# Up projection of the gated MLP by Strassen's scheme: seven block products, two phases of 1024 tokens, and normed rows that pass through DRAM

## The reference

```python
mix = (gates[..., :D_MODEL] * y_a + gates[..., D_MODEL:] * y_b) @ w_out[l]
h = h + _rms_norm(mix, norm_mix_post[l])
hn = _rms_norm(h, norm_ffn_pre[l])
up = hn @ ffn_w_up[l]                                  # (2064, 1024) @ (1024, 5632)
a = _causal_dwconv(up[..., :D_FF], ffn_conv_w[l], ffn_conv_b[l])   # 3 taps over tokens
f = (jax.nn.gelu(a, approximate=True) * up[..., D_FF:]) @ ffn_w_down[l]
h = h + _rms_norm(f, norm_ffn_post[l])
return h[:, N_META:, :]
```

## Time and profile before

| | |
|---|---|
| Median of 3 runs | 3570.68 us (3565.49 to 3570.95) |
| Span of the profiled execution, first to last instruction | 3565.1 us |
| What lies around the span | not printed by itself; against the three runs, 0.4 to 5.9 us |
| PE busy | 3324.0 us, 93% of the span |
| PEld busy | 2995.8 us, 84% |
| DVE busy | 1443.1 us, 40% |
| ACT busy | 994.6 us, 28% |
| Mean granted clock of TensorE | 0.965 of 2.4 GHz |
| up stage | from 2073 us to 3067 us of the span |

### The profile page before, as it was taken

The page is one execution under the profiler, slowest core; times in us unless marked ns, Lnnn a source line. Parts: engine busy times, 40 slices in busy tenths (PEclk is TensorE's granted clock), DMA queues, the critical chain, the costliest instruction groups (busy, mean ns, idle before and its releaser), DMA issues. The chain is left out here.

```text
span 3565.1 us, 67387 instructions
## 1 busy us (share of the span) xinstructions
PE 3324.0 (93%) x26926; PEld 2995.8 (84%) x26926; DVE 1443.1 (40%) x2535; ACT 994.6 (28%) x1549; POOL 121.3 (3%) x126
## 2 busy tenths in 40 slices
PE   6999999999775888869989989999999999999998
PEld 6999999999654777769988879999999999788887
DVE  6566642222295566654444442222222222311433
ACT  5211123343472444441113331111111111211311
POOL 0000000000001222210000000000000000000000
PEclk8999999999877999989999999999999999999999
DMA  5233344334484334333335411111111111311432
GB/s 158 88 122 114 114 138 125 121 123 127 148 291 118 89 91 96 86 132 127 101 123 147 124 66 47 47 47 47 47 47 47 47 47 38 139 49 49 136 117 93
DMA packets 300638, 357.67 MB, mean 100 GB/s; under 512 B 133600, under 2 KB 246112, under 8 KB 291856
## 3 DMA queue, kind: packets, MB, share of 16 engines
q1 hardware_dynamic: 300560, 356.59, 31.9%
HBM read 221.52 MB, written 135.00 MB: 100 GB/s over the span
## 5 line engine op out<-in xcount | busy, mean ns | idle before, releaser
L432 PE MATMUL psum<-x_hi,proj_w_hi 128*128 128x344 f32 x1632 | 534.9, 328 | 4.7 <-DVE proj_w_lo L519 4.7
L432 PE MATMUL psum<-x_lo,proj_w_hi 128*128 128x344 f32 x1632 | 525.2, 322 | 0.0
L432 PE MATMUL psum<-x_hi,proj_w_lo 128*128 128x344 f32 x1632 | 523.7, 321 | 0.0
L2381 PE MATMUL psum<-h_hi,up_w_hi 128*128 128x512 f32 (+2 forms) x1584 | 361.6, 370 | 6.8 <-ACT up_w_hi L2400 6.8
L2384 PE MATMUL psum<-h_lo,up_w_hi 128*128 128x512 f32 (+2 forms) x1584 | 361.7, 370 | 0.0
L2387 PE MATMUL psum<-h_hi,up_w_lo 128*128 128x512 f32 (+2 forms) x1584 | 360.5, 370 | 0.0
L2381 PEld LDWEIGHTS psum<-h_hi,up_w_hi 128*128 128x128 f32 x1584 | 297.4, 189 | 38.8 <-ACT up_w_hi L2400 6.9
L2384 PEld LDWEIGHTS psum<-h_lo,up_w_hi 128*128 128x128 f32 x1584 | 297.6, 188 | 32.4
L2387 PEld LDWEIGHTS psum<-h_hi,up_w_lo 128*128 128x128 f32 x1584 | 296.5, 188 | 32.2
L432 PEld LDWEIGHTS psum<-x_hi,proj_w_hi 128*128 128x128 f32 x1632 | 309.7, 190 | 6.2 <-issue 4.8
L432 PEld LDWEIGHTS psum<-x_lo,proj_w_hi 128*128 128x128 f32 x1632 | 309.4, 190 | 1.4
(11 more groups left out here) (314 smaller groups left out, 5141.2 us busy)
## 6 DMA issues: line engine op xcount, KB each, us to landing
up_weight<-in_w_up_tiles SPq DMA_DIRECT2D x44, 512.0 KB, 5.2
scratch_hidden<-up_hidden SPq DMA_DIRECT2D x22, 1024.0 KB, 4.1
down_a_raw<-scratch_hidden SPq DMA_DIRECT2D x32, 704.0 KB, 6.1
proj_area<-scratch_s_tab SPq DMA_DIRECT2D x32, 608.5 KB, 3.8
scratch_s_tab<-proj_area SPq DMA_DIRECT2D x16, 1089.0 KB, 4.3
proj_weight<-in_w_in_tiles SPq DMA_DIRECT2D x34, 512.0 KB, 4.1
scratch_gates<-proj_mixed SPq DMA_DIRECT2D x16, 1032.0 KB, 4.0
chunk_pre<-scratch_roles SPq DMA_DIRECT2D x128, 128.0 KB, 2.7
```

What stands on the lines that cost most here:

```text
L432: mm = nc.tensor.matmul(psum[:, bank(v, n), 0:N_TOK], w[:, v, k, :], x[:, k, cols], start=(k == 0 and w is w_hi and x is x_hi), stop=(k == ...
L2381: nc.tensor.matmul(out, w_hi[:, u, part, k, :], x_hi[:, k, cols], start=(k == 0), stop=False)
```

## The change

The up projection is now done in pairs of channel tiles. The normed activations are a 2 x 2 matrix of blocks: tokens in two halves, A11 and A12 for the first half (channels 0 to 511 and 512 to 1023), A21 and A22 for the second. A pair's weights are B11, B12, B21, B22 (two channel tiles by two halves of the 1024 inputs). Strassen's scheme in Winograd's form makes the four results from seven products:

P1 = A11 B11, P2 = A12 B21, P6 = S2 T2, P5 = S1 T1, P7 = S3 T3, P3 = S4 B22, P4 = A22 T4, with S1 = A21 + A22, S2 = S1 - A11, S3 = A11 - A21, S4 = A12 - S2, and four sums of weight blocks T1 to T4 (T3 in the place of B12). They are issued in this order. P1, P6, P7 and P4 add up in one PSUM bank (qa), P2 is alone in qb, P5 and P3 add up in qc; ACT copies the intermediate states P1, U2 (after P6), U3 (after P7) and P5 out, and DVE adds the results together.

A pair takes one unit of seven products for each block of columns of `a` and one for `b`. There are two phases of 1024 tokens: in the first the columns of `a` are 256 and 258 (the last two are the tokens ahead of the sequence), in the second 512; `b` is 512 in both. All weights are loaded, summed and split once per phase.

The normed rows of mixout go to DRAM and not to SBUF (`next_rows`, `store_next`). After the twelfth tile's loads, SP brings the first 1024 tokens back in 16 DMAs of 256 KB, and the first weight set of 1 MB; the other 1024 tokens are loaded by `ffn_up` in the last pair of phase one.

The diff, cut to its core (m is the pair, s the weight set, u the unit):

```diff
 # token_projection, SyncE
+            def row_tiles(i, first_next):
                 for u in range(SLOTS):
                     r = 2 * i + u
                     load_acts(part, r, P, r * P)
                     load_rows(r, u, P, r * P)
                     store(r - 2, u, P, (r - 2) * P)
+                    if next_norm and (first_next or u):
+                        store_next(r - 3, 1 - u)
...
+                READY = 6
+                row_tiles(1, False)
+                with sp.Fori(2, READY) as i:
+                    row_tiles(i, True)
+                for u in range(SLOTS):
+                    sp.wait_ge(next_stored[u], 16 * ((2 * UP_COLS // P) // 2) + 16)
+                for n, (quarter, k, at_t) in enumerate(((0, 0, 0), (1, 0, UP_COLS), (2, K4, UP_COLS), (3, K4, 0))):
+                    for r in range(UP_COLS // P):
+                        sp.dma_start(next_first[quarter][:, :, r * P:(r + 1) * P], next_x[at_t // P + r, :, k:k + K4]).then_inc(next_loaded, 16)
+                for buffer, source, sem in next_loads:
+                    sp.dma_start(buffer, source).then_inc(sem, 16)
+                with sp.Fori(READY, TILES // 2) as i:
+                    row_tiles(i, True)
...
+                store_next(TILES - 1, 1)
...
 # ffn_up, TensorE
+            def unit(phase, u, s, banks, cols, free_a, free_b, free_c):
+                qa, qb, qc = (psum[:, b, 0:cols.stop - cols.start] for b in banks)
+                for j, (out, opens, closes) in enumerate(((qa, True, False), (qb, True, True), (qa, False, False), (qc, True, False), (qa, False, False), (qc, False, True), (qa, False, True))):
...
+                    for before, copied in ((P_6, p1_copied), (P_7, u2_copied), (P_3, p5_copied), (P_4, u3_copied)):
+                        if j == before:
+                            pe.wait_ge(copied, u + 1)
+                    pe.wait_ge(w_hi_ready, 7 * s + j + 1)
+                    pe.wait_ge(x_hi_ready[j], phase + 1)
+                    for k in range(K4):
+                        nc.tensor.matmul(out, w_hi[:, j, k, :], x_hi(phase, j)[:, k, cols], start=opens and k == 0, stop=False, skip_group_check=True)
+                    pe.wait_ge(w_lo_ready, 7 * s + j + 1)
+                    for k in range(K4):
+                        nc.tensor.matmul(out, w_lo[:, j, k, :], x_hi(phase, j)[:, k, cols], start=False, stop=False, skip_group_check=True)
+                    pe.wait_ge(x_lo_ready[j], phase + 1)
+                    for k in range(K4):
+                        mm = nc.tensor.matmul(out, w_hi[:, j, k, :], x_lo(phase, j)[:, k, cols], start=False, stop=closes and k == K4 - 1, skip_group_check=True)
+                    mm.then_inc(product_done[j], 1)
...
 # ffn_up, ScalarE
+            x_high(FIRST, OP_A11)
+            high(0, 0, 0, None, 0)
+            high(0, 0, 1, None, 0)
+            x_high(FIRST, OP_A12)
+            x_high(FIRST, OP_S1)
+            x_high(FIRST, OP_S2)
+            for j in range(2, 7):
+                high(0, 0, j, None, 0)
+            for op in (OP_S3, OP_A22, OP_S4):
+                x_high(FIRST, op)
...
+                # b unit of a pair; in x_high, S4 waits for x_lo_ready[A22]
+                copied(p1, 6, P_1, p1_copied, u, (c11_done, u + 3), UP_COLS)
+                split(0)
+                split(1)
+                copied(u2, 6, P_6, u2_copied, u, (c12_done, u + 3), UP_COLS)
+                gelu(g, 0)
+                gelu(g, 1)
+                split(2)
+                copied(p5, 2, P_5, p5_copied, u, (c22_done, u), UP_COLS)
+                split(3)
+                copied(u3, 6, P_7, u3_copied, u, (c22_done, u), UP_COLS)
+                split(4)
+                if last and phase == FIRST:
+                    x_high(SECOND, OP_A11)
+                    x_high(SECOND, OP_A12)
+                split(5)
+                split(6)
+                if last and phase == FIRST:
+                    for op in (OP_S1, OP_S2, OP_S3, OP_A22, OP_S4):
+                        x_high(SECOND, op)
...
 # ffn_up, VectorE
+            x_sum(FIRST, OP_S1)
+            low(0, 0, 0)
+            x_low(FIRST, OP_A11)
+            low(0, 0, 1)
+            x_sum(FIRST, OP_S2)
+            x_low(FIRST, OP_A12)
+            x_sum(FIRST, OP_S4)
+            sums(0, 0, 0)
+            low(0, 0, 2)
+            x_low(FIRST, OP_S2)
+            low(0, 0, 3)
+            x_low(FIRST, OP_S1)
+            x_sum(FIRST, OP_S3)
+            for j in (4, 5, 6):
+                low(0, 0, j)
+            for op in (OP_S3, OP_A22, OP_S4):
+                x_low(FIRST, op)
...
+                # b unit, last pair of phase one
+                if last and phase == FIRST:
+                    x_low(SECOND, OP_A11)
+                    x_low(SECOND, OP_A12)
...
+                if last and phase == FIRST:
+                    for which in (OP_S1, OP_S2, OP_S4):
+                        x_sum(SECOND, which)
+                    x_low(SECOND, OP_S2)
+                    x_sum(SECOND, OP_S3)
+                    for op in (OP_S1, OP_S3, OP_A22, OP_S4):
+                        x_low(SECOND, op)
```

More of the change, by code:

```diff
@@ L58 @@
 M_FF = D_FF // P
+UP_COLS = 512
+UP_ROW = 528
 K4 = RWKV_WIDTH // P
@@ new lines, in pair @@
+            def pair(phase, m, last):
+                g, n = pair_of(phase, m), n_parts(phase)
+                for part, (c0, c1) in enumerate(a_parts(phase)):
+                    u, a = units_before(phase, m) + part, a_before(phase, m) + part
+                    back = 3 if phase == FIRST else 2
+                    unit(phase, u, 2 * g, (3 * part, 3 * part + 1, 3 * part + 2), slice(c0, c1),
+                         (c21_copied, a - 1 + 2 if phase == FIRST else a + 2), (c11_done, u + 1 - back + 3), (c12_done, u + 3 if part == 0 else u - 2 + 3))
+                u = units_before(phase, m) + n
+                unit(phase, u, 2 * g + 1, (6, 7, 2), slice(0, UP_COLS), (b_used, 4 * g + 4), (c11_done, u + 1 - (n + 1) + 3), (c12_done, u + 1 - n + 3))
@@ L2418, in _, with copied, high @@
-            tile_loop(act, tile)
+            def copied(dst, bank, j, sem, u, free, width):
+                act.wait_ge(product_done[j], u + 1)
+                act.wait_ge(*free)
+                nc.scalar.activation(dst[:, 0:width], psum[:, bank, 0:width], ACT.Copy).then_inc(sem, 1)
+            def high(s, part, j, units, count):
+                if j == 0:
+                    act.wait_ge(*((first_set_loaded, 16) if part == 0 and isinstance(count, int) and count == 0 else (weight_loaded[part], 16 * count + (0 if part == 0 else 16))))
+                if j in (2, 3, 4, 6):
+                    act.wait_ge(t_ready, 4 * s + {2: 2, 3: 1, 4: 3, 6: 4}[j])
+                if units is not None:
+                    act.wait_ge(product_done[j], units)
+                nc.scalar.activation(w_hi[:, j], weight_of(part, j), ACT.Copy).then_inc(w_hi_ready, 1)
@@ L2420, in _ @@
+            phases(act, pair)
         @block.vector
         def _(dve):
-            dve.sem_inc(split_lo, 2)
-            dve.sem_inc(conv_done, 1)
-            dve.sem_inc(b_used, B_BLOCKS)
-            def split(m, i, u, part):
-                if isinstance(i, int) and i > LAST:
-                    return
-                dve.wait_ge(split_hi, 2 * m + part + 1)
-                nc.vector.tensor_tensor(w_lo[:, u, part], weight[:, part], w_hi[:, u, part].bitcast(F32), ALU.subtract).then_inc(split_lo, 1)
@@ L2461, in hybrid_block @@
+            phases(dve, pair)
 def hybrid_block(nc, ins, out):
```

461 lines of the change are left out of this document (311 added, 150 removed).

## The result

The changed kernel takes 3517.15 us (median of 4 runs, 3514.36 to 3524.07) against 3569.68 for the kernel before on the same chip: ratio 0.9856, 95% interval 0.9844 to 0.9869. Forecast were 3517 us, and a change of -53.8 us against the profiled span; the span went from 3565.1 to 3513.9 us, -51.2. The sum is right within 3 us; its terms are off by up to 6 us, and cancel. That the median meets the forecast to the microsecond is luck.

What follows compares the result with a forecast made beforehand. The prediction took TensorE (PE), through the number and length of its matmuls, to bound the up stage. Terms: -118.6 + 2 + 25.1 + 25.4 + 8 + 4.3 = -53.8 us, from 3570.7 to 3517 us; 8-in-10 range 3485 to 3560.

Steps and rivals of the forecast that it cites:

- Products: Up stage: 4620 matmuls in place of 4752, many half as long, 866.8 us against 985.4: -118.6 us.
- (a): Up stage: matmuls no cheaper below 344 columns, 157 ns, +66 us, 3583 us; chance 0.10, two cycles a column included.
- (b): Up stage: weight load and matmul in series for narrow matmuls, 295 ns, +321 us, 3838 us; chance 0.02.
- Inside a pair: Up stage, each pair: PE waits for other engines; P3 in the B unit fits by 0.1 us; charged +2 us.
- at the loop's end it is hidden: Up stage, loop's end: table load of 1.28 us no cost; P1's copy ends by 2.5, P6 due at 2.9 us.
- rival (c): Up stage: a wait inside every pair, +1 to 2 us each, 3542 to 3562 us; chance 0.14.
- Start of the stage: Up stage's start: P6 can't start until 33.2 us in, behind P1's copy on ACT; +25.1 us, bounds 20 to 30.
- Between the phases: Up stage, start of phase two: P6 starts at 28.4 us in place of 5.6, cold restart 2.5: +25.4 us.
- the chain: Up stage, phase two's start: P6 waits for P1's copy, behind S4's conversion, behind A22's low part; P6 at 28.4 us.
- The burst: Mixout stage, tile 12: activations land behind 16 loads and weights; stall 5.0, cold restart 2.5: +8 us, bounds 0, 24.
- The stage's end: End of the mixout stage: last store goes late, and SP waits 4.9 us until it has landed: +4.3 us.
- rival (d): Up stage: 512 columns at 225.7 ns (-16); mixout burst hidden (-8): 3493 us; or two gaps shorter; chance 0.12.

Runs made afterwards that it cites:

- Experiment 10: Column blocks of a in phase one made 128 and 386 wide in place of 256 and 258, against the changed kernel: 3618.78 us.
- experiment 2: GELU's table loaded once by its own instruction at the up stage's head, against the changed kernel: 3509.47 us, ratio 0.9832.
- Experiment 3: ACT's copies put between the conversions in each phase's first unit, first pair outside the loop, against the changed kernel: 3495.99 us, ratio 0.9798.
- experiment 1: The burst of 16 activation loads spread over tiles 12 to 15, weight set behind them, against the changed kernel: 3505.24 us, ratio 0.9818.

## Why the prediction was right, point by point

- **Products:** forecast -118.6 us, measured 924 x (0.1175 + 0.1201) + 2772 x 0.2317 - 985.4 = -123.6. The mechanism, columns and some 11 to 18 ns beside them, held; 256 and 258 columns were mis-sized by 3.5 and 2 ns. Rivals (a), 157 ns, and (b), 295 ns, are refuted. Experiment 10 shows that (a) had a core: there is such a step, but below 256 columns, not below 344. The rule of the Trainium skill (TensorE: Matmul & The Clock Gate, Part 3, The mechanism) that a load overlaps matmuls in flight only when row groups differ, with the estimate of 213 ns that the prediction drew from it for 256 columns, finds no support at the widths measured here.
- **Inside a pair:** forecast +2 us from P3 in the B unit. There is no wait there: the copy of P5 ends before P3's start at 2233.30. The step that failed is "at the loop's end it is hidden". I let the table load run as soon as ACT was free; in the trace it starts only after P1 is complete (its row names PE as what ended the wait before it), in series with the copy. Measured: 9 x 0.86 = +7.7 us; experiment 2 takes it away. It is a wait of the kind of rival (c), at less than its lower price of 1 us a pair and in nine pairs only.
- **Start of the stage:** forecast +25.1. The first unit takes 42.2 us, 84 x 0.1175 = 9.9 would do, so 32.3 are lost, against 7.7 before: +24.6. A table load of 1.28 us that I had missed is made up by VectorE's pieces, which follow one another a little closer than their lengths, and by a restart of 1.7 us (four groups from 2120.00 to 2123.55, 3.55 us for 1.88) in place of 2.5.
- **Between the phases:** forecast +25.4. P6 was due at 2565.85 and started at 2589.24, 23.4; the four groups behind it took 6.24 us for 3.71, 2.5: +25.9. Right in both parts, though the loads came later than the forecast had them: A12's conversion waited 2.0 us for one (until 2559.83), and the sums began 7.9 us into the phase, not 7.5. Experiment 3 shows that P1's copy stood where the chain put it, but also that the chain's order explains less than half of the loss: without it 9.7 of the 25.9 us come back.
- **The burst:** forecast +8, measured 9.9 and a restart of 1.6 to 1.7 us (8 matmuls at 0.426 in place of 0.226): +11.5, which experiment 1 gives back as 11.9. The term was mis-sized: tile 12's activations were in use at 2011.8 where I had 2008.0, 23.2 us after the burst began and not 18.9. SyncE is held for 14.3 us by the 17 issues, and the load behind them takes 8.4 us to land, where I gave it 3. In the terms of the forecast: it let the bytes flow from the first issue on, and the first load of the burst lands only after 3.9 us; and the stretch from 1988 to 2016 us moved 298 GB/s, not 330. These two explain most of the 4 us (an estimate: 3.9 us, and then the other 5.5 MB at 298 GB/s, are 22.4 of the 23.2 us); the issues need not be a cost of their own.
- **The stage's end:** forecast +4.3. From VectorE's last row to the next stage's first conversion it was 1.3 us before (2071.97 to 2073.24 in the earlier trace rows) and is 4.1 after (2082.47 to 2086.57): +2.8. The store lands 2.7 us after its issue at 2082.26, where I had 4.9, and the next stage begins 1.6 us behind that, where I had 0.9, for which the forecast names no row.
- **Sum:** -123.6 + 7.7 + 24.6 + 25.9 + 11.5 + 2.8 = -51.1 us; the spans differ by 51.2. By stages: the up stage is 65.2 us shorter (terms: 65.4), mixout from its first matmul to the up stage 14.5 longer (terms: 14.3), and the rest of the span, which the change does not touch, 0.6 shorter. So the terms hold to some 0.3 us, and the last 0.1 is chance.

Of rival (d) nothing came: 512 columns kept 231.7 ns, in both orders and with changing banks, the burst was not hidden, and the gaps were not shorter. Why 512 columns take 225.7 ns in the down stage stays open; where the operands lie was not tried.

## What to carry to other kernels

When an algorithm with fewer products sends intermediate results through another engine, count where each copy stands in that engine's program in the *first* unit, behind the preparation of all operands: here PE stood over 20 us twice, and copies between the conversions gave back 14 us of it. The same edit took the table loads out of the loop, 8 us more, and spreading one burst of loads gave 12, for 3480 us in place of 3517 and 3570. Peel or preload for activation tables, because a load at a loop's head runs behind the first wait and not under it. Cost a burst of DMAs from its first issue to the landing of the load that stands behind it in the queue: latency first, then all bytes at the rate that the burst itself reaches (here 3.9 us and some 300 GB/s).

## What was not expected of the hardware

- VectorE and GpSimd exclude one another for whole instructions: 0.68 us became 4.90 beside a GpSimd sum.
- A row of issues holds SyncE longer than one: for loads of 256 KB in 512-byte pieces 0.40 us for the first of a row, 0.67 as the mean of 4 and 0.84 as the mean of 16; a 1 MB load that takes 0.35 us by itself took 0.83 behind them.
- Matmuls of this type hardly get cheaper from 256 (117.5 ns) to 128 columns (111 ns). In eight of ten narrow units TensorE's granted clock fell from 1.00 to 0.51, though PE had stood for no more than 0.6 us in them; in the one unit without that wait it did not fall.
